# A hybrid attention step on one core: the stick mask added by TensorE, bias masked in two tiles, one kept buffer handed from stage to stage

## The reference, cut to what matters

```
p = rmsnorm(x) @ w_in                            # 2048 -> 7510 columns: q, k, v, gates of all kinds
cmp = silu((blocks of 32 keys + pe) @ w1) @ w2   # compressed keys and values of NSA
# stick breaking:
log_keep = where(k_pos < q_pos, log_sigmoid(-z), 0);  log_after = reverse cumsum - log_keep
a = where(k_pos < q_pos, exp(log_sigmoid(z) + log_after), 0)
# dsa: index scores relu(iq @ ik) * iw, top 256 keys, masked_softmax(q @ k + bias) @ v
# nsa: o = g0 * cmp attention + g1 * attention to the 16 best blocks of 64 + g2 * window of 512
y = x + rmsnorm((o * silu(gate)) @ w_out)
```

## Time and profile before

| | us |
|---|---|
| median of 3 runs | 2711.36 (2710.96 to 2715.70) |
| the profiled execution's own time | 2711.83 |
| its span, first to last instruction | 2710.1 |
| PE busy, share of the span | 2327.8 (86%) |
| DVE busy | 1018.2 (38%) |
| ACT busy | 757.2 (28%) |
| POOL busy | 513.2 (19%) |

### The profile page before, as it was taken

How to read it: one execution, slowest core, us unless ns; L and a number is a source line. 1 busy time by engine, 2 the same in 40 slices (tenths; PEclk the granted TensorE clock), 3 DMA queues, 4 the chain that set the end, 5 groups by cost and what they waited for, 6 DMA issues and landing times. The chain is left out here.

```text
span 2710.1 us, 45261 instructions
## 1 busy us (share of the span) xinstructions
PE 2327.8 (86%) x16097; PEld 1762.2 (65%) x16097; DVE 1018.2 (38%) x1706; ACT 757.2 (28%) x1706; POOL 513.2 (19%) x350
## 2 busy tenths in 40 slices
PE   5999999999994998996688878888699765898996
PEld 3888888888884998996245544444355543676884
DVE  5111011011001222222358857667533346986122
ACT  4000000000001222221034444455355464453010
POOL 6433333333315000000000000000000003344331
PEclk7999999999996999997899979999899876898998
DMA  5323333333329878661689989999899763003223
GB/s 177 134 98 112 105 101 112 101 104 112 112 110 251 246 239 222 205 197 32 119 276 353 358 283 396 393 383 395 269 341 379 277 190 128 1 2 125 78 86 116
DMA packets 344748, 522.93 MB, mean 193 GB/s; under 512 B 67741, under 2 KB 151086, under 8 KB 342142
## 3 DMA queue, kind: packets, MB, share of 16 engines
q1 hardware_dynamic: 313866, 492.02, 54.5%
q10 hardware_dynamic: 27984, 23.13, 2.9%
q0 software_dynamic: 2704, 5.33, 0.6%
HBM read 498.09 MB, written 44.00 MB: 200 GB/s over the span
## 5 line engine op out<-in xcount | busy, mean ns | idle before, releaser
L461 PE MATMUL proj_acc<-proj_w_hi,h_hi 128*128 128x512 f32 (+1 forms) x960 | 370.0, 385 | 8.5 <-POOL proj_w_lo L430 8.5
L462 PE MATMUL proj_acc<-proj_w_hi,h_lo 128*128 128x512 f32 (+1 forms) x960 | 370.1, 386 | 0.0
L463 PE MATMUL proj_acc<-proj_w_lo,h_hi 128*128 128x512 f32 (+1 forms) x960 | 369.6, 385 | 0.0
L430 POOL TENSOR_TENSOR proj_w_lo<-w_in,proj_w_hi 128x2048 fp32r<-128x2048 f32 (+1 forms) x60 | 272.8, 4549 | 459.1 <-DVE proj_w_hi L399 459.1
L782 PE MATMUL cmp_hp<-cmp_xT,cmp_w 128*128 128x128 f32 x2048 | 252.5, 277 | 12.2 <-DVE cmp_xT L813 12.2
L399 DVE CAST proj_w_hi<-w_in 128x2048 fp32r<-128x2048 f32 (+1 forms) x60 | 80.7, 1349 | 466.7 <-PE proj_acc L454 463.9
L782 PEld LDWEIGHTS cmp_hp<-cmp_xT,cmp_w 128*128 128x128 f32 x2048 | 240.5, 193 | 16.3 <-DVE cmp_xT L813 15.9
L485 ACT COPY proj_out<-proj_acc 128x512 f32<-128x512 f32 (+1 forms) x60 | 34.7, 579 | 697.4 <-PE proj_acc L463 697.4
L1299 PE MATMUL sb_tp<-kept_consts,kept_rows 128*128 128x128 f32 x1024 | 165.0, 309 | 52.2 <-DMA kept_rows<-in_cache_sb_kv_dram 34.5
L461 PEld LDWEIGHTS proj_acc<-proj_w_hi,h_hi 128*128 128x128 f32 x960 | 180.8, 188 | 44.4 <-issue 8.8
L1299 PEld LDWEIGHTS sb_tp<-kept_consts,kept_rows 128*128 128x128 f32 x1024 | 123.4, 155 | 124.8 <-ACT sb_kT L1441 61.0
(11 more groups left out here) (411 smaller groups left out, 3547.7 us busy)
## 6 DMA issues: line engine op xcount, KB each, us to landing
kept_rows<-in_cache_sb_kv_dram SPq DMA_DIRECT2D x320, 256.0 KB, 6.1
cmp_rows<-in_cache_nsa_kv_dram SPq DMA_DIRECT2D x512, 128.0 KB, 2.4
kept_rows<-in_cache_nsa_kv_dram SPq DMA_DIRECT2D x256, 256.0 KB, 5.0
kept_rows<-in_cache_dsa_kv_dram SPq DMA_DIRECT2D x256, 256.0 KB, 4.8
w_in<-in_w_in_dram SPq DMA_DIRECT2D x56, 1024.0 KB, 5.0
sb_v_rows<-in_cache_sb_kv_dram SPq DMA_DIRECT2D x192, 256.0 KB, 6.3
fin_w<-in_w_out_dram SPq DMA_DIRECT2D x32, 512.0 KB, 3.7
proj<-proj_out ACTq DMA_DIRECT2D x14, 1024.0 KB, 4.4
```

The source lines that it names most:

```text
L430: pool.tensor_tensor(w_lo[q][:, :, 0:width], w[q][:, :, 0:width], w_hi[q][:, :, 0:width], ALU.subtract).then_inc(lo_made, 1)
L461: pe.matmul(to, h_hi[:, kk, r], w_hi[q][:, k, 0:width], start=(kk == 0), stop=False)
L462: pe.matmul(to, h_lo[:, kk, r], w_hi[q][:, k, 0:width], start=False, stop=False)
L463: last = pe.matmul(to, h_hi[:, kk, r], w_lo[q][:, k, 0:width], start=False, stop=(kk == KT_IN - 1))
```

## The change

- One buffer `region` of four times 2048 columns lives through the whole kernel. It is in turn the weights `w` of the projection, the weights of the keys `w1_keys` of the compression, the rows of the index keys and two of the four slots `kept.rows`, and at the end `kept.oT`.
- `w1_keys` is asked for in `project_in`, behind the state's copy: its first half once POOL has done with pieces 0 and 1 of the last group, the second with all four. `compress` no longer asks for it.
- The index keys' rows of chunk 0 (all) and chunk 1 (SP's half) are asked for in `cmp_sample`; SP gives 32 DMAs from its start, ACT 16 after its last copy.
- The selected stream has two steps asked for ahead in place of three (`ready=2`); the third is asked for at its start.
- In the preparation SP asks for `gate_s` ahead of piece 8, for the bias of heads 6 to 11 in one DMA ahead of piece 10 and of heads 0 to 5 ahead of piece 15. DVE adds the mask to the tiles of 128 columns in which it is not zero (three additions of 6 heads by 128 columns) and takes the tile maxima in one reduction, joined by three small steps.
- In the attention POOL's additions and DVE's 24 reductions are gone. A stick unit's mask is added by PE: a bf16 product of 128 columns with the identity puts -1e30 on the masked scores, and both triangle products and an empty instruction of DVE are gone. ACT's last exp of a stick unit stands one unit later in its order. Of the copies DVE keeps those of u divisible by 3 from unit 16 on, which there are the short "cmp" units, and ACT takes the others; stick units alternate as before.

```diff
@@ project_in
             sp.dma_start(io.win_s[:, 0:WIN - NT, :], io.win_state[:, NT:WIN, :]).then_inc(state_copied, 16)
+            for a in range(2):
+                sp.wait_ge(lo_made, whole * 4 + 2 * a + 2 + 4)
+                sp.dma_start(kept.w1_keys[:, a], io.cmp_w1[a]).then_inc(kept.w1_keys_in, 16)
             sp.wait_ge(state_copied, 16)
@@ compress
-            for a in range(2):
-                sp.dma_start(w1[:, a], io.cmp_w1[a]).then_inc(w1_in[0], 16)
@@ index_scores
-            for c in range(NCH):
+            for c in range(2, NCH):
                 load(sp, mybir.EngineType.SP, 0, c)
-                if c == 0:
+                if c == 2:
                     sp.wait_ge(bias_zeroed, 1)
                     load_bias(sp, io, kept.bias_nsa, 6, 0, kept.bias_nsa_in)
-            for n in range(AHEAD):
+            for n in range(2):
                 step_rows(sp, nc, io, kept, "slc", io.nsa_cache, 512, n, lambda n: None)
...
-            for c in range(NCH):
+            for c in range(1, NCH):
                 load(act, mybir.EngineType.Activation, 4, c)
@@ cmp_sample
+        @block.sync
+        def _(sp):
+            for c in range(2):
+                index_load(sp, mybir.EngineType.SP, nc, io, kept, 0, c, lambda b: None)
...
             act.copy(pT[:], tp[:]).then_inc(copied, 1)
+            index_load(act, mybir.EngineType.Activation, nc, io, kept, 4, 0, lambda b: None)
@@ prompt_prepare
+                if i == 8:
+                    (the three DMAs of gate_s)
+                if i in (10, 15):
+                    first = 6 if i == 10 else 0
+                    src = bass.AP(io.lines.tensor, P - 1 + first * XL, [[HB * XL - 1, P], [XL, 6], [1, XW]])
+                    sp.dma_start(kept.bias[:, first:first + 6, :], src).then_inc(bias_in[i // 15], 16)
...
+            def mask(first, at):
+                dve.wait_ge(bias_in[0 if first else 1], 16)
+                b = kept.bias[:, first:first + 6, at:at + P]
+                dve.tensor_tensor(b, b, pm[:, at:at + P].unsqueeze(1).to_broadcast([P, 6, P]), ALU.add).then_inc(biased, 1)
             def gate(i, n):
+                if n == 13:
+                    mask(6, 0)
+                    mask(6, SEQ)
+                if n == 15:
+                    mask(0, SEQ)
+                if n == 16:
+                    dve.wait_ge(biased, 1)
+                    own = kept.bias[:, 6:12, 0:SEQ].rearrange("p h (j c) -> p h j c", c=P)
+                    dve.tensor_reduce(kept.pad_least[:], own, AX.X, ALU.max, negate=True).then_inc(pad_step, 1)
@@ prompt_attention
+        by_act = [u % 2 if u < n_stick else int(u % 3 > 0) for u in range(N)]
...
-                pe.matmul(sc[x.u % SB][:, 0:x.w], q, kept.kT[:, x.k, 0:x.w], start=not dropping, stop=True).then_inc(scored, 1)
+                masked = x.kind == "stick"
+                last = pe.matmul(sc[x.u % SB][:, 0:x.w], q, kept.kT[:, x.k, 0:x.w], start=not dropping, stop=not masked)
+                if masked:
+                    last = pe.matmul(sc[x.u % SB][:, x.w - P:x.w], kept.ident_b[:], kept.dropp[:, 0, 0:P], start=False, stop=True)
+                last.then_inc(scored, 1)
...
-            for n, first in enumerate((6, 9, 0, 3)):
-                pool.wait_ge(kept.bias_in, 64)
-                for h in range(first, first + 3):
-                    b = kept.bias[:, h, :]
-                    pool.tensor_tensor(b, b, kept.pmask[:, 0:XW], ALU.add).then_inc(biased, 1)
...
-                if 1 <= u <= n_stick:
+                if 2 <= u <= n_stick:
+                    exp_stick(units[u - 2])
+                if u == n_stick:
                     exp_stick(units[u - 1])
...
-                    d = softs[x.u % 2][:, x.w - P:x.w]
-                    dve.tensor_tensor(d, d, tri, ALU.mult).then_inc(soft_dve, 1)
...
-                    d = view(x)[:, x.w - P:x.w]
-                    dve.tensor_tensor(d, d, tri, ALU.mult).then_inc(ready_stick, 1)
```

More of the change, by code:

```diff
@@ L541, in step_rows, with index_rows, index_load @@
     for b in range(2):
-        to = kept.rows[n % 4][:].rearrange("p (b m c) -> p b m c", b=2, m=PPC)[:, b]
+        to = kept.rows[n % 4].rearrange("p (b m c) -> p b m c", b=2, m=PPC)[:, b]
         load_pages(sp, pages[b * PPC:(b + 1) * PPC], to, cache, col, 4 * DH, kept.arrived[tag][n % 4][b])
+INDEX_BUF = 3
+def index_rows(kept, c):
+    return kept.region[:, c % INDEX_BUF * 2048:(c % INDEX_BUF + 1) * 2048].rearrange("p (b q d) -> p b q d", b=NB, q=PPC)
+def index_load(eng, engine, nc, io, kept, first, c, free):
+    pages = page_numbers(nc, io, kept.by_chunk, (c * NB + first) * PPC, 4 * PPC, engine)
+    for b in range(first, first + 4):
+        free(b)
+        load_pages(eng, pages[(b - first) * PPC:(b - first + 1) * PPC], index_rows(kept, c)[:, b], io.idx_cache, 0, 64, kept.arrived["idx"][c % INDEX_BUF][b])
 def key_place(kept, m):
@@ L720, in few_products @@
             def few_products(e):
[L722 removed]
+                pe.wait_ge(w1_values_in if e else kept.w1_keys_in, 32)
                 pe.wait_ge(x_copied[0], e + 1)
@@ L939, in index_scores @@
         s = Scope(nc, ctx, "idx")
-        BUF, TB = 3, 4
-        rows = [s.sb(f"rows{i}", [P, NB, PPC, 64]) for i in range(BUF)]
+        BUF, TB = INDEX_BUF, 4
+        rows = [index_rows(kept, c) for c in range(BUF)]
         kT = [s.sb(f"kT{b}", [P, 2, P]) for b in range(NB)]
@@ L946, in index_scores @@
         total = s.ps("total", [NS, CH])
-        rows_in = [[s.sem(f"rows_in{i}_{b}") for b in range(NB)] for i in range(BUF)]
+        rows_in = kept.arrived["idx"]
         turned, copied, multiplied = s.sem("turned"), s.sem("copied"), s.sem("multiplied")
@@ L1106, in stream @@
         else:
-            rows = [kept.rows[i][:].rearrange("p (b m c) -> p b m c", b=per, m=PPC) for i in range(SLOTS)]
+            rows = [kept.rows[i].rearrange("p (b m c) -> p b m c", b=per, m=PPC) for i in range(SLOTS)]
             k_rows = [r[:, :, :, 0:width] for r in rows]
@@ L1822, in slc_sample @@
            select=kept.sel_e, dropped_keys=keys, bias=lambda lo, hi: kept.bias_nsa[:, lo:hi], bias_in=(kept.bias_nsa_in, 64),
-           ahead=ahead, head0=10, gate=1, add=True,
+           ready=2, ahead=ahead, head0=10, gate=1, add=True,
            rounds=range(SLC_ROUNDS))
@@ L2057, in _ @@
             dve.reciprocal(kept.pgates[:], kept.pgates[:]).then_inc(gated, 1)
+            for j in range(1, 4):
+                dve.wait_ge(pad_step, j)
+                least = kept.pad_least[:, :, j:j + 1]
+                dve.tensor_tensor(least, least, kept.pad_least[:, :, j - 1:j], ALU.min).then_inc(pad_step, 1)
+            tri = kept.pmask[:, C_TRI - C_PM:C_TRI - C_PM + P]
+            dve.tensor_scalar(kept.dropp[:, 0, 0:P], tri, -NEG, NEG, ALU.mult, ALU.add).then_inc(biased, 1)
 class Unit:
@@ L2134, in prompt_attention, with wait_copied @@
         ops_until = lambda u: min(n_ops, (u + 1) * n_ops // (n_free - 4))
+        by_act = [u % 2 if u < n_stick else int(u % 3 > 0) for u in range(N)]
+        def wait_copied(eng, u):
+            eng.wait_ge(copied[by_act[u]], sum(by_act[v] == by_act[u] for v in range(u + 1)))
         def padded_before(x):
@@ L2153, in score @@
                     if before.kind == "stick":
-                        pe.wait_ge(added, before.u + 1)
+                        pe.wait_ge(soft_dve, 3 * before.u + 3)
                     else:
@@ L2286, in _ @@
             chain = Links(small)
-            tri = kept.pmask[:, C_TRI - C_PM:C_TRI - C_PM + P]
             dve.wait_ge(cleared, LB)
-            pad_step = {}
-            def pad(h, i):
-                pad_step[h, i] = chain.step(dve.tensor_reduce(pad_max[:, h, i:i + 1], kept.bias[:, 6 + h, 0:SEQ - i * P], AX.X, ALU.max, negate=True))
             def add(x):
@@ L2617, in program @@
             place_queries(kept, sample)
+            kept.arrived = {"idx": [[sample.sem(f"idx_in{i}_{b}") for b in range(NB)] for i in range(INDEX_BUF)]}
             kept.drop_blk = sample.sb("drop_blk", [P, NSB], BF16)
```

112 lines of the change are left out of this document (48 added, 64 removed).

## The result

The changed kernel takes 2666.84 us (median of 4 runs, 2664.37 to 2668.66), the kernel before 2711.16 in the same series: ratio 0.9833, 95% interval 0.9816 to 0.985, so 44 us or 1.7% faster. The forecast was 2666.

The account below looks back on a forecast made before the run. Bounds differ by stage: PE and SP's queue in the compression, DVE in the attention, no engine full in the preparation. Terms -16.8 - 6 + 0 + 3.1 - 17 - 8.5 = -45.2 us gave 2666 against the median, range 2652 to 2684.

Parts of the forecast that it names:

- Part 1: Compression: requesting the keys' weights earlier lets SP reach the pages 16.9 us earlier; gain 16.8 us, bounds 12.3 and 18.
- The page turn: Compression: PE's first turn of the second half's pages comes near 861 in place of 877.7.
- Part 2: Index stage: fewer ACT requests ahead of its first total, and an earlier barrier; gain 6 us, bounds 2 and 10.
- Part 3: Selected stream: one step less asked for ahead costs nothing; 5 us if the cover were gone.
- Part 4: Preparation: gate_s wait saved, pieces delayed, DVE work added; sum +3.1 us, bounds -5 to +8.
- Rival B: Preparation: ACT's backlog covers the pieces, which are not held up; -5 us there, 2658 in all; chance 0.15.
- about 8 of it at the stage's end: Preparation: late pieces cost PE 11.3 us, about 8 at the end, since ACT works off gates in each stall.
- Part 5: Stick units: DVE loses 18.6 us of triangle products, reductions and slowing by POOL; gain 17 us, bounds 12 and 20.
- Part 6: Slc, win and cmp units: DVE falls to 76.9 us, PE's floor is 84.6; stage 89.5, gain 8.5 us.
- rival A: Slc, win and cmp units stay bound by the chain; gain there 0 to 2, 2674 to 2675 in all; chance 0.17.
- rival D: Attention: TensorE stays at 0.50 clock through slc, win and cmp units; +80 us, 2746 in all; chance 0.02.
- Rival C: Compression: the keys' weights queue behind the state's copy and come too late; 2683 in all; chance 0.03.

Follow-up runs that it names:

- keys_late: Changed kernel with the weights of the keys asked for in the compression again, ahead of w2: 2683.39 us, ratio to before 0.989.
- take_early: Changed kernel with ACT taking the total of chunk c - 2, not c - 3, behind its requests for chunk c: 2669.08 us, ratio to before 0.9834.
- stick_index: Changed kernel with ACT making all stick-unit copies, earlier index totals and 16 of ACT's last index requests moved to SP: 2658.0 us, ratio to before 0.98.
- index_late: Changed kernel with all index rows asked for in the index stage again: 2675.93 us, ratio to before 0.9866.
- stick_mask_order: Changed kernel with the stick triangle multiplied in by DVE again and ACT's exponential one unit behind, as before: 2676.79 us, ratio to before 0.9862.
- bias_after_pieces: Changed kernel with both bias transfers behind the last piece, masks and reduction at the preparation's end: 2670.03 us, ratio to before 0.9837.

## Why the prediction was right, and where inside it was not

**Part 1** (forecast -16.8, measured -16.7; the twelve kernels with the early request average -15.6, and undoing it cost 18 to 19). The step "the pages begin near 822.5" came at 822.4 and "few_products moves to 830.2" at 830.3. The page turn was put at 861 and came at 863.9: the pages of the second half were asked for 16.6 us earlier (849.7 in place of 866.3), nearly the whole shift, but TensorE had the first of them 14.2 us after that in place of 11.4. The shift there is 13.8 us; the 2.5 us that complete the stage's gain are TensorE's busy time, 382.5 to 380.0 in the stage, at a clock of 0.97 in place of 0.95. The forecast has no such term, so that the number was met to 0.1 us is luck. The clock is not chance alone, though: it was 0.949 in the two kernels with the late request (before and keys_late) and 0.959 to 0.973 in the twelve with the early one.

**Part 2** (forecast -6, measured -5.8, by the undone part -4.9). The first copy of a total was put at 1291 and came at 1292.4. What the forecast took for granted, that ACT's pace bounds what follows, is what take_early and stick_index showed. The first copy is only a mark for it: moved by 9.9 us alone it gave 1.5, while the 16 requests that ACT no longer has to give in the index stage took 9.4 us off it. The other half of the sum, a barrier 4 to 5 us later, measured 3.6, but mostly by the clock (see index_late) and not by the issues alone.

**Part 3** (0): the selected stream took 209.1 us before and 208.9 after.

**Part 4** (forecast +3.1, measured +3.2). The three waits for pieces were put at 2.6, 5.8 less 1.3, and 4.2 us for pieces 8, 10 and 15, and measured 3.5, 3.0 and 5.7: 12.2 together where 11.3 were worked out, and some 10 if the small waits for pieces that they replace (1.3, 0.7 and 0.6 us before) are taken off. The other terms fit: an addition took 0.95 us (0.8 to 1.1 forecast), the reduction 3.34 us (3.1 to 4.4), and the return of the gate_s wait costs 6.9. TensorE's last product ended 66.3 us into the stage in place of 65.1, and what is left behind it took 7.9 us in place of 5.9, so that its end moved by 1.2 and the rest by 2.0 us, against 0.9 and 2.2 in the forecast. Rival B is refuted: the pieces were held up. But the step "about 8 of it at the stage's end" was right only in sum. Without the two behind the bias TensorE got to its last transposes only 1.2 us earlier, because it then ran at the lower level.

**Part 5** (forecast -17, measured -20.6). The term was mis-sized. DVE's busy time fell by 18.0 us (57.6 to 39.6), with 18.6 forecast, though in other shares: 11.2 for the two triangle products (9.9 forecast from 328 and 292 ns; over all units they took 341 and 382), 4.8 in the scans, 1.9 for the four reductions, which came off as worked out. The 328 ns were not undisturbed: eleven of those twelve operations took 291 or 292 ns and one, beside POOL's last addition, 729. With 291 and 279 ns (stick_mask_order) the products themselves are 9.1 us, and about 2 of the 11.2 are POOL's doing. The allowance of 1.6 us for new waits of DVE for ACT was wrong in sign: its idle time fell from 6.8 to 4.3 us. Of that 2.5 us the runs explain nothing: it was 4.5 with the masks on DVE and 4.1 with POOL's additions, each alone. Nor do the parts add up: the masks (8.1), the additions (3.8) and the reductions (1.9 by their busy time) come to 13.8 of the 20.6 us. Some 3 more are triangle products and scans that POOL held in the kernel before and that no single run brings back together; the masks and the additions undone in one kernel were not run. This stays open.

**Part 6** (forecast -8.5, measured -6.7). TensorE is the next bound, as said, by its 87.6 of 90.8 us, at 1.00 of its clock; rival A (the chain stays the bound) and rival D (the low level) are refuted. The floor was mis-sized: its work was put at 84.6 us and is 87.6, and the 3.2 us above it are less than the 4.9 allowed. DVE was put at 76.9 us and shows 80.9: its reductions and copies fell by 16.8 us, counted one by one (9.3 of reductions, copies from 14.1 to 6.6), its busy time by 12.7 (93.6 to 80.9), since neighbours on one engine overlap in the records: all of DVE's durations in the stretch, added one by one, come to 119.4 us before and 103.3 after. Of DVE's two savings the new division of the copies is worth 1.6 us, by its own run. The rest goes with the reductions, which were not undone alone, and part of it, 2 us at most, can be the clock. In the first 4 us of this stretch the kernel before had TensorE at 0.50 and never idle, the changed one had 1.00 there:

```profile
2326.00:2330.00 4.00, 4.00 (x19) 3.71 (x18) 4.00 (x17) 1.78 (x6) 0.44 (x1) 0.50 0.00 0
```

**Rival C** did not happen: the weights were there at 830, and few_products waited for nothing.

So the total of 2666 was met because each term came within 4 us, with part 5 too small by 3.6, part 6 too large by 1.8, and 1.6 us in the finish that lie within its spread. That the median came within 1 us of the forecast is luck: in the profiled executions the stages give 47.6 us where 45.2 were worked out, and single runs of the changed kernel lie 4.3 us apart.

## What to carry to other kernels

Cut the kernel at its barriers, price each edit in the stage it is made in, and ask who is the next bound there: 12.7 us less on DVE gave 6.7, with TensorE right behind. The stream of small requests here was bounded by the engines that issue them, at 0.50 to 0.63 us each, and moving the issues to a queue with room gained more (5.4 us) than moving the waits (1.5). And when a mask is moved to another engine, look again at the order in which a third one works: the same two operations cost 8.1 or 16.3 us.

## What the runs showed of the hardware

```profile
2265.29 1.64 DVE L2309 TENSOR_TENSOR_SCAN pa_soft<-pa_soft 128x128 f32<-128x128 f32 x1
...
2278.72 2.44 DVE L2309 TENSOR_TENSOR_SCAN pa_soft<-pa_soft 128x512 f32<-128x512 f32 x1
```

Over the sixteen units the triangle products rose from 291 and 279 ns on average (stick_mask_order) to 341 and 382 (before). The operations with one input in PSUM took 491 and 477 or 478 ns with and without them, and the maxima 551 and 549. The Trainium skill, "SBUF — State Buffer", the section on who interferes with whom, says that DVE and GpSimd share one pair of ports as an exclusive lock, which a DVE operation with two SBUF inputs needs against a GpSimd one that reads SBUF. By this rule exactly these operations are held, and the trace agrees.

TensorE stayed at 0.50 of its clock through 17 us in which it was busy without a gap (2218 to 2235 in bias_after_pieces), after ten in which it was busy for 7.05 us at 0.91. The Trainium skill, "TensorE: Matmul & The Clock Gate", Part 1, says that the clock is throttled by default and that activity releases it; by this rule the order with fewer stalls should have had the higher level, and in two profiles out of two it had the lower one.
